# Differential attention: value's second half among the first units, bias sum and maximum in one instruction, output product in halves of its contraction

## What is computed

```
proj = h @ w_in                       # h = rms_norm(x); q, k, v of 1024 columns each
q = rms_norm(q per head half) * 64**-0.5 ; k = rms_norm(k per head half)
for each of 2 query blocks of 128 rows, each of 8 heads:
    p1 = softmax(q1 @ k1.T + bias) ; p2 = softmax(q2 @ k2.T + bias)
    out = (p1 - lam * p2) @ v         # 128 x 256 by 256 x 128
out = rms_norm(out per head) * (1 - lam_init)
x = x + out @ w_out                   # 1024 x 1024
```

## Time and profile before

| | |
|---|---|
| median of 3 runs (lowest, highest) | 2024.37 us (2019.29, 2025.61) |
| the profiled execution, its own time | 2024.16 us |
| span of its trace | 2022.4 us |
| busy: PE, PEld, DVE, ACT | 1924.5, 1613.5, 1226.9, 992.1 us |
| chain that ended last, by engine | PE 86%, DVE 8%, ACT 3%, issue 2% |

### The profile page before, as it was taken

The page is one execution under the profiler, slowest core; times in us unless marked ns, Lnnn a source line. Parts: engine busy times, 40 slices in busy tenths (PEclk is TensorE's granted clock), DMA queues, the critical chain, the costliest instruction groups (busy, mean ns, idle before and its releaser), DMA issues.

```text
span 2022.4 us, 26323 instructions
## 1 busy us (share of the span) xinstructions
PE 1924.5 (95%) x9384; PEld 1613.5 (80%) x9384; DVE 1226.9 (61%) x1633; ACT 992.1 (49%) x1479; POOL 64.2 (3%) x94
## 2 busy tenths in 40 slices
PE   9999989999999998799999999978989999989998
PEld 7887777888788886688888887867878788878886
DVE  5554786555555578655555566887565556655564
ACT  5444665544544455654453546633355543334444
POOL 1000000000000000000000001010000012100000
PEclk9999999999999999999999999989989999999999
DMA  7656334666685653166565555422135544336453
GB/s 224 188 185 185 120 115 153 184 188 188 189 257 186 186 172 125 57 184 182 189 200 167 183 167 176 148 77 70 40 107 170 159 146 126 104 105 210 153 187 115
DMA packets 215891, 316.88 MB, mean 157 GB/s; under 512 B 16658, under 2 KB 115208, under 8 KB 215536
## 3 DMA queue, kind: packets, MB, share of 16 engines
q1 hardware_dynamic: 212704, 306.76, 49.2%
q0 software_dynamic: 3024, 8.75, 1.3%
q10 hardware_dynamic: 64, 0.02, 0.0%
HBM read 314.41 MB, written 3.16 MB: 157 GB/s over the span
## 4 chain that ended last, share of the span: by engine, by line
PE 86%; DVE 8%; ACT 3%; issue 2%; DMA 0%; SPq 0%; DVEq 0%; ACTq 0%
PE acc L754 50%; PE acc L759 24%; PE tp L714 4%; DVE w_lo L1998 1%; PE tp L1163 1%; PE tp L870 1%; PE mx L1163 1%; DVE arena L2478 1%; ACT w_hi L1381 1%; DVE arena L2242 1%; PE mx L1302 1%; PE mx L1303 1%; DVE x L2069 1%; DVE arena L2402 1%; PE mx L1218 0%
## 5 line engine op out<-in xcount | busy, mean ns | idle before, releaser
L1998 DVE TENSOR_TENSOR w_lo<-w_raw,w_hi 128x1024 fp32r<-128x1024 f32 (+1 forms) x589 | 712.6, 1217 | 518.3 <-ACT w_hi L1381 516.3
L1381 ACT ACTIVATE w_hi<-w_raw 128x1024 fp32r<-128x1024 f32 (+1 forms) x589 | 612.9, 1048 | 568.7 <-PE acc L759 546.7
L754 PE MATMUL acc<-w_hi,norm_hi 128*128 128x512 f32 x1488 | 475.0, 401 | 4.1 <-DVE norm_lo L2017 3.5
L754 PE MATMUL acc<-w_hi,norm_lo 128*128 128x512 f32 x1488 | 461.8, 392 | 0.0
L759 PE MATMUL acc<-w_lo,norm_hi 128*128 128x512 f32 x1488 | 396.4, 389 | 0.0
L754 PEld LDWEIGHTS acc<-w_hi,norm_lo 128*128 128x128 f32 x1488 | 281.6, 190 | 59.8
L759 PEld LDWEIGHTS acc<-w_lo,norm_hi 128*128 128x128 f32 x1488 | 278.8, 188 | 58.0
L754 PEld LDWEIGHTS acc<-w_hi,norm_hi 128*128 128x128 f32 x1488 | 274.2, 191 | 58.9 <-issue 3.1
L754 PE MATMUL acc<-w_hi,inner_hi 128*128 128x512 f32 (+1 forms) x864 | 267.3, 391 | 4.0 <-DVE inner_lo L2017 2.5
L754 PE MATMUL acc<-w_hi,inner_lo 128*128 128x512 f32 (+1 forms) x864 | 262.9, 386 | 0.0
L759 PE MATMUL acc<-w_lo,inner_hi 128*128 128x512 f32 (+1 forms) x864 | 226.9, 385 | 0.0
(11 more groups left out here) (309 smaller groups left out, 1351.5 us busy)
## 6 DMA issues: line engine op xcount, KB each, us to landing
w_raw<-in_ffn_w_gu SPq DMA_DIRECT2D x352, 256.0 KB, 3.0
w_raw<-in_ffn_w_down SPq DMA_DIRECT2D x88, 512.0 KB, 4.6
w_raw<-in_pool_w_in SPq DMA_DIRECT2D x64, 512.0 KB, 3.8
w_raw<-in_gdn_w_in SPq DMA_DIRECT2D x48, 512.0 KB, 3.9
w_raw<-in_pool_w_out SPq DMA_DIRECT2D x32, 512.0 KB, 4.4
w_raw<-in_mla_w_in SPq DMA_DIRECT2D x26, 512.0 KB, 3.7
w_raw<-in_gla_w_in SPq DMA_DIRECT2D x24, 512.0 KB, 3.6
w_raw<-in_diff_w_in SPq DMA_DIRECT2D x24, 512.0 KB, 4.3
```

Of the source, the lines that this page charges most:

```text
L754: pe.matmul(acc_of(g, i, part, tok, 0, w), t[:, tile * SEQ + tok * P:tile * SEQ + (tok + 1) * P], b_hi, start=t is hi and k + kk == 0, sto ...
L1381: act.activation(slot(w_hi, g, i, p, 0, n), slot(w_raw, g, i, p, 0, n), ACT.Copy).then_inc(S["rounded"], 1)
L1998: dve.tensor_tensor(slot(w_lo, g, i, p, 0, n), slot(w_raw, g, i, p, 0, n), slot(w_hi, g, i, p, 0, n).bitcast(F32), ALU.subtract).then_inc( ...
```

## The change

Four things, all in `diff`:

1. Value's second block is no longer multiplied before the units. Its first chunk stands behind `scores(0)` and `scores(1)`, its other three in the loop of units at n = 1, 3 and 5, ahead of that unit's transposes; ACT takes it at n = 6. It keeps two banks of `acc` until then, so the units have one bank for transposed probabilities and one for values (the pair of the block that is taken), and change to the other pair at n = 8. ACT and DVE treat one weight chunk each behind their first units and at n = 1, 3 and 5.
2. `take_scores` is two instructions of 256 columns, each of which adds the bias, negates, writes the sum and keeps the minimum. Scores have two banks (both of `mx`) and stand two units ahead, not three; ACT runs `exps(n + 2)` behind `take_o(n - 1)`.
3. The norm over a head runs in two halves, heads 0 to 3 and 4 to 7. The root of the first is taken at n = 14, with the load of the function table that it needs; a load of the table for the exponential is set ahead of the taking of value's first block.
4. The product with `w_out` is one gemm with two parts and its chunks in the order of the contraction: four chunks over heads 0 to 3 (both column blocks), then the transposes of heads 4 to 7, then four chunks over those heads. The transposes of `x` stand behind the seventh chunk.

```diff
+        if turn_by is not None:
+            self.chunks.sort(key=lambda c: (c[1] // turn_by, c[0], c[1]))
...
-            linear("diff.out", t["diff_w_out"][0], KD, BANK, TT, 2)]
+            halves("diff.out", t["diff_w_out"][0], KD, BANK, 2, KD // 2)]
...
         def diff_bank(n):
-            return bank(mx, n % 4) if n % 4 < 2 else bank(tp, n % 4 - 2)
+            return bank(mx, n % 2)
+        def diff_pt_bank(n):
+            return bank(acc, 2 * G["diff.v"].odd(int(n >= diff_half)), 0, SEQ)
+        def diff_o_bank(n):
+            return bank(acc, 2 * G["diff.v"].odd(int(n >= diff_half)) + 1, 0, P)
...
                 turned(last_turn)
                 pe.wait_ge(S["diff_vec_ready"], 1)
-                wait_evacuated(pe, v_g, 1)
-                for n in range(DIFF_AHEAD - 1):
-                    scores(n)
-                for n in range(len(units)):
-                    if n + DIFF_AHEAD - 1 < len(units):
-                        scores(n + DIFF_AHEAD - 1)
+                scores(0)
+                scores(1)
+                product(v_g, 1, norm_t, only=0)
+                wait_evacuated(pe, v_g, 0)
+                for n in range(2 * diff_half):
+                    if n + 2 < 2 * diff_half:
+                        scores(n + 2)
+                    if n in (1, 3, 5):
+                        product(v_g, 1, norm_t, only=(n + 1) // 2)
+                    if n == diff_half:
+                        wait_evacuated(pe, v_g, 1)
                     probs_turned(n)
                     if n:
                         values(n - 1)
...
-                for u in range(4):
-                    turn_tokens(qk, DM, 2 * u)
-                finish(out_g, inner_t, need=last_of(u0))
+                turn_heads(0)
+                for p_n in range(2):
+                    product(out_g, 0, inner_t, part=0, only=p_n, need=need_heads)
+                product(out_g, 0, inner_t, part=1, only=2, need=need_heads)
+                product(out_g, 0, inner_t, part=1, only=3, need=need_heads)
+                turn_heads(1)
+                finish_halves(out_g, inner_t, need_heads)
...
+                act.activation(warm[:, :], eps[:, :], ACT.Exp)
+                feed.before_evac(v_g, 0)
...
-                see["diff_o_taken"].wait(act)
-                see["diff_o_root"].up(act.activation(stat[:, 48:64], stat[:, 32:48], ACT.Sqrt, bias=eps[:, :], scale=1.0 / P))
+                    if n == 6:
+                        scaled_evac(v_g, 1, diff_t["v"], DM, ACT.Copy)
+                    if n == 14:
+                        act.activation(warm[:, :], eps[:, :], ACT.Sqrt)
+                        root(0)
+                take_o(2 * diff_half - 1)
+                root(1)
...
-                    see["diff_s_taken"].up(dve.tensor_tensor(dst, diff_bank(n).rearrange("p (m k) -> p m k", m=2),
-                                                             b.to_broadcast([P, 2, SEQ]), ALU.add))
-                    see["diff_s_taken"].wait(dve)
-                    see["diff_max_ready"].up(dve.tensor_reduce(stat[:, 16 + 2 * ring:18 + 2 * ring], dst, AX_X, ALU.max, negate=True))
+                    for m in range(2):
+                        last = dve.tensor_tensor_reduce(out=s[:, ring * BANK + m * SEQ:ring * BANK + (m + 1) * SEQ],
+                                                        in0=diff_bank(n)[:, m * SEQ:(m + 1) * SEQ], in1=b, scale=-1.0, scalar=3.0e38,
+                                                        op0=ALU.add, op1=ALU.min, accum_out=stat[:, 16 + 2 * ring + m:17 + 2 * ring + m])
+                    see["diff_s_taken"].up(last)
...
+                take_scores(0)
+                take_scores(1)
+                probs(0)
+                feed.to(v_g.chunk(1, 0) + HEAD + 1)
+                for n in range(2 * diff_half):
+                    if n + 2 < 2 * diff_half:
+                        take_scores(n + 2)
+                    if n in (1, 3, 5):
+                        feed.to(v_g.chunk(1, (n + 1) // 2) + HEAD + 1)
+                    if n + 1 < 2 * diff_half:
+                        probs(n + 1)
+                normed(0)
+                for u in range(2):
+                    lo_part(inner_t, 2 * u, lambda k: ROWS["subln"])
+                feed.to(out_g.chunk0 + 4)
+                normed(1)
+                feed.to(out_g.chunk0 + 7)
```

More of the change, by code:

```diff
@@ L819, in finish, with finish_halves @@
                 product(g, 1, xt, between=lambda p: turn_x(st, (0, 1)) if p == 1 and st else None)
+            def finish_halves(g, xt, need):
+                st = following.get(g.name.split(".")[0])
+                for p in (g.n // 2, g.n // 2 + 1):
+                    product(g, 0, xt, part=0, only=p, need=need)
+                product(g, 0, xt, part=1, only=g.n - 2, need=need)
+                if st:
+                    turn_x(st, (0, 1))
+                product(g, 0, xt, part=1, only=g.n - 1, need=need)
             def last_of(u0):
```

150 lines of the change are left out of this document (85 added, 65 removed).

## The result

The changed kernel takes 2013.72 us (median of 8 executions, 2009.99 to 2016.31), the kernel before on the same chips 2021.8 us: ratio 0.9956, 95% interval 0.9941 to 0.9971, 8 to 9 us faster. The forecast was 2016.5 us, in a range from 2012.5 to 2023.0, with "faster by over 0.3%" at 0.61. On another chip, beside the last experiments, the same changed kernel gave 2011.07 us and 0.9927 (0.9912 to 0.9941). Medians and ratios here are of executions that agree; one execution of `idle_heads`, at 4576.11 us, stands far apart and is left out.

The account below looks back on a forecast made before the run. TensorE was taken as the bound, with holes in units VectorE paced at 2.36 us. A new timetable of the stage ended at 855.9 against 863.5, 7.6 us less: 2024.16 to 2016.5 us, range 2012.5 to 2023.

Parts of the forecast that it names:

- the two new waits: TensorE idle 3.1 us ahead of the first scores and 1.5 us between the halves of the output product.
- the rival to which 0.04 was given: Clock does not fall and the kept value's read is hidden, a half 0.46 us: 2013.5 us; chance 0.04.
- units 6 to 13: Units after value's chunks: eight at 2.14 us, 17.1, plus 0.6 for late ScalarE work, to 822.6.
- the last two units: From unit 14's transposes at 822.6 through ScalarE's work and table load to the last value product at 826.6.
- First scores: Before the units: 3.1 us wait for the last keys, then 1.5 us lost to a low clock, to 785.0.
- Units 0 to 5: Units with three value chunks: 18.4 us of TensorE work plus 1.5 for low parts, to 804.9.
- The fused instruction: Bias sum with maximum on VectorE: 0.55 us a half, 0.46 to 0.64; a unit 2.14 instead of 2.36.
- The scan rival: Fused instruction at the scan's rate, 0.82 us a half, VectorE 2.68 a unit: 2023.4 us; chance 0.14.
- the two-pass rival: Each fused half makes the sum, then runs over it again, 1.11 us a half: 2032 us; chance 0.04.
- Two banks of scores: In the units: round of transposes, values and scores takes 2.1 us, about as long as VectorE's 2.14.
- The table load: In the last two units on ScalarE: 1.3 us, costing 1.6; the skill's drain would add 1.4 to the sum.
- The output product: Two times four chunks with a 1.5 us gap between, 0.4 for a first chunk partly at lower clock, to 855.9.

Follow-up runs that it names:

- idle_heads: Changed kernel with useless small products added where TensorE waits at the end of the units: 2014.45 us, ratio 0.9956.
- keys_first: Changed kernel with the last keys transposed a chunk earlier and copied behind one low part instead of four: 2009.83 us, ratio 0.9924.
- fused_alone: Kernel before with only bias sum and maximum made one instruction a map, four score banks kept: 2016.25 us, ratio 0.9954.
- v_before_units: Changed kernel with value's second block multiplied whole ahead of the units again: 2008.24 us, ratio 0.9930.
- keys_and_gap: Changed kernel with last keys a chunk earlier and second heads' transposes ahead of the output product's fourth chunk: 2004.62 us, ratio 0.9901.
- after_again: The changed kernel measured once more without any edit, on another chip: 2011.07 us, ratio 0.9927.

## Why the prediction held, and which of its steps did not

The sign and the range came out, and so did the two new waits and the low clock behind the first. What paces the units did not: they ran at 1.95 us where 2.1 to 2.2 was named as the sign of being right, and the fused instruction at 0.35 where 0.55 was. The time is 2.8 us under the forecast, in which errors in one direction stand against one in the other; that it lies on the 2013.5 of the rival to which 0.04 was given is chance, since that rival wanted a hidden read, which came, and a clock that does not fall, which fell twice. Forecast and trace, step by step:

| step | forecast, us | profiled | difference |
|---|---|---|---|
| stage's start to the third unit's scores | to 785.0 | 785.29 | +0.3 |
| to the transposes of unit 6 | 19.9 | 17.99 | -1.9 |
| units 6 to 13 | 17.7 | 15.62 | -2.1 |
| the last two units | 4.0 | 4.00 | 0 |
| to the output product | 3.8 | 3.98 | +0.2 |
| to the next product | 25.5 | 27.58 | +2.1 |
| end | 855.9 | 854.46 | -1.4 |

The remaining 1.1 us of the span's 10.2 lie outside the stage, where the instructions are the same; no run explains them.

*First scores.* Right in both terms: a wait of 2.86 for the keys where 3.1 was put, and a low clock behind it. `keys_first` priced the two together at 4.6, by taking them away.

*Units 0 to 5.* The 18.4 of TensorE's own work was right to 0.4; the 1.5 for low parts ahead of the first probabilities was not needed, since TensorE worked without a hole from 782 to 803.3.

*The fused instruction.* The term that was mis-sized. A half costs 0.35 where I took 0.55, below even my lower bound of 0.46. A nearer row than the two that I took stood in the earlier trace rows: the bias addition, with the same sources, 0.72 from start to start for both halves, so 0.36 for one. The fused instruction goes at the pace of the plain addition, and the maximum comes with it. I had built it from a 480 ns instruction and a 155 ns read; the custom operation lasts 0.42, and the read's 0.08 lies wholly beside the next instruction. The scan rival and the two-pass rival fall with it. The Trainium skill's rule of the halved rate ("Vector Engine (DVE) Microarchitecture Reference", Points that are easy to get wrong) asks for two SBUF sources; with one in PSUM, as here, no halving shows. No run had both in SBUF, and no trace tells whether this custom operation falls under that rule.

*Two banks of scores.* The step that failed. I wrote that the round of transposes, values and scores takes 2.1 us, "so TensorE's side of the round is as long as VectorE's, and a cheaper fused instruction gains next to nothing here". The rows of `fused_alone` (four banks, 1.77 a unit) and `v_before_units` (two banks, 25.5 us for fourteen units, 787.73 to 813.22, 1.82 a unit) show a round below 1.83 with two banks. What holds the units is ScalarE, 1.83 to 1.85 us of its own instructions a unit against the 1.92 that I had in the prices and did not carry into the pace. This is read from rows (ScalarE busy 19.21 of 19.60 us); no run shortened ScalarE's work.

*What this hid.* My sum had value's chunks at "its 8.2 here and none of it lies in a hole of the old kind", weighed against the 11.2 of the old place, and never against the hole that the fused instruction closes. The 2 x 2 of runs shows it (stage in us, and in brackets the clock of the output product's first chunk; norm and output product in halves in all):

| | value's block ahead of the units | among the units |
|---|---|---|
| old pair | 86.3 (low) | 84.5 (low) |
| fused | 74.5 (full) | 79.3 (low), 77.3 (full) |

So in the stage the fused instruction alone brings 9.9 us, as much as the whole change. The halves of the norm bring 3 to 4, the halves of the contraction none. Value's move costs 3 with the wait in front of it, and with the shorter wait of `keys_and_gap` it comes out even. That the sum agreed with the measured time to 3 us says little on the parts.

*The table load.* The next instruction starts 1.29 us behind it (820.38 to 821.67), as in the earlier trace rows, and the last value product stood 4.00 behind the transposes of unit 14, as forecast. The Trainium skill's drain of 1.38 us ("ScalarE: Activation LUTs", What ACT_TABLE_LOAD costs) did not show here either.

*The output product.* The gap of 1.50 was exact. The clock was not: 0.4 forecast, 2.2 measured (first chunk 4.95 instead of 2.72), and in `after_again` 0.1. Both belonged in the range; I had taken the first chunk of the kernel before as wholly at the lower clock, but it took 3.56, only 0.84 more than 2.72, while 4.95 is what a first chunk costs here when the low clock lasts.

## What to carry over

When two edits both live on one engine's idle time, price each with the other in place: an edit that shortens the loop takes away the room that the other fills, and four runs, each with and without, show it where a single sum does not. For a loop with several engines write down each one's own work a round (here VectorE 2.36, ScalarE 1.83, TensorE 1.6 to 1.7): the gain of speeding up the first ends at the second. And before work is moved away from in front of a consumer, look for the copy that it hid; moving that copy one chunk earlier was worth 2.7 us at like clocks, about what value's move had cost. Last, set the ends of a measured stretch where no edit reaches: measured from its own last transposes, `keys_first` would seem 2.2 us better than it is, since its new waits lie ahead of them and between them.

## What the runs showed of the hardware

- An addition with a kept minimum over 128x256 f32, one source in PSUM: 0.42 us long, 0.35 from start to start with its read of 0.08. A two-tensor instruction with a scalar lasts 480 ns at that size, and the plain addition of the same sources takes 0.36 for as many columns. I had expected the accumulating form to be dearer; it costs the same as the plain addition.
- The granted clock behind the same waits differs between executions: of one kernel's two profiles one had 0.61 over the 4.4 us ahead of the output product and 1.00 behind, the other 0.50 over 4.8 us and then 0.53 for 5 us, a difference of 2.1 us in one chunk. Over all kernels the first chunk took 2.8 us in seven profiles and 3.3 to 5.1 in the other seven. With TensorE kept busy (`idle_heads`) the clock did not fall. What decides between the two was not settled.
